# Attention score matmuls of two heads issued alternately, in pairs of tiles, with norm sums and scores sharing three PSUM banks

## The reference

```
h = RMSNorm(x);   q/k/v of all groups, z_A, z_B, g_A, g_B = split(h @ w_in)
q, k: RMS norm per head (64 wide)
Mixer A: 3 groups x 8 heads, query t reads t - j*d, j = 0..window/d, (window, d) = (128,1), (512,4), (2048,16)
         the three group outputs are added with weights proportional to their softmax denominators
Mixer B: 8 query heads, 2 kv heads, query t reads t-128..t, one sink logit per head in the denominator
scores = q.k / 8 - slope * distance;  p = softmax(scores);  o = p @ v
y = x + W_out( sig(g_A) * (o_A * silu(z_A)) @ P_A + sig(g_B) * (o_B * silu(z_B)) @ P_B )
```

## Time and profile before

| | |
|---|---|
| runs of the kernel before | 2306.69, 2309.11 and 2353.67 us, median 2309.11 us |
| the profiled execution's own time | 2317.27 us |
| span of its slowest core (core 3) | 2315.7 us |
| spans of the eight cores | 2283.2 to 2315.7 us |
| busy on core 3: PE, DVE, ACT, POOL | 1887.8, 1258.6, 1226.0, 428.7 us |
| mean granted TensorE clock, core 3 | 0.913 of full speed |

### The profile page before, as it was taken

How to read it: one execution, slowest core, us unless ns; L and a number is a source line. 1 busy time by engine, 2 the same in 40 slices (tenths; PEclk the granted TensorE clock), 3 DMA queues, 4 the chain that set the end, 5 groups by cost and what they waited for, 6 DMA issues and landing times.

```text
span 2315.7 us, 43826 instructions; the slowest of 8 cores (2283.2 to 2315.7 us)
## 1 busy us (share of the span) xinstructions
PE 1887.8 (82%) x14352; PEld 1073.0 (46%) x14352; DVE 1258.6 (54%) x1948; ACT 1226.0 (53%) x2190; POOL 428.7 (19%) x519
## 2 busy tenths in 40 slices
PE   3676576798698987988889887785786999999995
PEld 1453453464455544555555544342333445444442
DVE  3454254545355553554545545664565677776773
ACT  3544365577476864767657766775787311111110
POOL 0122001112112130121311212321222111111110
PEclk8798778899899998999999998887898999999997
DMA  7498753599757896659964696779455568777764
GB/s 171 130 227 198 141 163 104 146 185 183 170 143 166 177 181 163 167 139 203 181 160 153 163 193 128 155 152 164 124 132 136 171 189 232 218 214 199 200 174 128
DMA packets 133998, 389.20 MB, mean 168 GB/s; under 512 B 15488, under 2 KB 87696, under 8 KB 129520
## 3 DMA queue, kind: packets, MB, share of 16 engines
q10 hardware_dynamic: 5680, 178.06, 33.4%
q1 hardware_dynamic: 97024, 119.95, 19.3%
q0 software_dynamic: 31072, 88.39, 18.6%
HBM read 363.23 MB, written 230.06 MB: 256 GB/s over the span
## 4 chain that ended last, share of the span: by engine, by line
PE 56%; ACT 14%; DMA 13%; issue 9%; DVE 6%; ACTq 1%; POOL 1%; DVEq 0%; SPq 0%; POOLq 0%
PE ps L53 56%; ACT nl L53 6%; DMA xT<-scr_x 4%; DMA rw<-win 3%; ACT expt L53 2%; DMA sa<-ra 2%; ACT sq L53 2%; ACT ld L53 1%; ACT rb L53 1%; DVE tt L53 1%; DVE rd L53 1%; DVE pt L53 1%; DVE ra L53 1%; DMA ld<-x 1%; DVE rb L53 1%
## 5 line engine op out<-in xcount | busy, mean ns | idle before, releaser
L53 PE MATMUL ps<-xT,rw 128*128 128x512 bf16 x2496 | 672.9, 406 | 27.8 <-DMA xT<-scr_x 21.4
L53 DVE TENSOR_TENSOR pt<-expt,mask 128x512 bf16<-128x512 f32 x512 | 388.7, 772 | 273.8 <-ACT expt L53 249.8
L53 ACT ACTIVATE expt<-ps 128x512 f32<-128x512 f32 x576 | 334.3, 595 | 156.1 <-PE ps L53 117.0
L53 PEld LDWEIGHTS ps<-xT,rw 128*128 128x128 bf16 x2496 | 252.9, 106 | 286.1 <-issue 87.2
L53 PE MATMUL ps<-ra,rd 64*128 64x128 bf16 (+2 forms) x1792 | 281.2, 280 | 93.3 <-ACT expt L53 52.6
L53 ACT ACTIVATE sq<-ps 128x512 bf16<-128x512 f32 x257 | 149.3, 581 | 237.5 <-PE ps L53 237.2
L53 ACT ACTIVATE nl<-ps,epsS 128x512 f32<-128x512 f32 x257 | 174.9, 680 | 154.4 <-PE ps L53 150.1
L53 PE MATMUL ps<-rw,xT 128*128 128x128 bf16 x3328 | 228.9, 228 | 28.5 <-DMA rw<-win 15.9
L53 PEld LDWEIGHTS ps<-ra,rd 64*128 64x128 bf16 (+1 forms) x1792 | 127.8, 102 | 267.2 <-issue 202.6
L53 PEld LDWEIGHTS ps<-rw,xT 128*128 128x128 bf16 x3328 | 217.3, 122 | 36.9 <-issue 30.2
L53 ACT ACTIVATE nl<-nl 128x512 f32<-128x512 f32 (+1 forms) x321 | 200.8, 626 | 29.8
(11 more groups left out here) (134 smaller groups left out, 2212.3 us busy)
## 6 DMA issues: line engine op xcount, KB each, us to landing
xT<-scr_x SPq DMA_DIRECT2D x40, 1024.0 KB, 10.9
sa<-ca ACTq DMA_DIRECT2D x32, 1020.0 KB, 10.1
ra<-ca POOLq DMA_DIRECT2D x48, 512.0 KB, 6.9
rw<-win POOLq DMA_DIRECT2D x78, 256.0 KB, 14.8
rb<-x SPq DMA_DIRECT2D x32, 512.0 KB, 6.2
rb<-xh SPq DMA_DIRECT2D x16, 512.0 KB, 8.8
scr_x<-xT POOLq DMA_DIRECT2D x8, 1024.0 KB, 10.0
scr_ab<-ra SPq DMA_DIRECT2D x64, 128.0 KB, 4.8
```

Of the source, the lines that this page charges most:

```text
L53: return lambda eng: getattr(eng, name)(*args, **kwargs)
```

## The change

The score matmuls of a tile become a list of single steps (`s_mm`), and Exp and mask multiplication a separate part (`s_post`). `pair_heads` reorders each group's tiles so that tile i of head 0 and tile i of head 1 are neighbours in A. `do_tile` now issues two tiles at a time: their score matmuls in turn (head 0, head 1, head 0, ...), then both Exp and mask operations, then the `pv` parts with `LAG = 2`, which are those of the pair before. The planner deals out pairs (the account may reach 4, and 2 are taken off at a time). The norm sums and the scores take their banks from one rotation of the banks 3, 4 and 5, and the merge units keep the banks 4 and 5 in a rotation of their own.

```diff
-    rPJ = Rot([0, 1, 2]); NB = 3; rST = Rot([4, 5]); UA, UB = 6, 7
+    rPJ = Rot([0, 1, 2]); rST = Rot([3, 4, 5]); rMG = Rot([4, 5]); UA, UB = 6, 7
...
-            si, ni, b0 = st_["si"], rNL.next(), bank[0]
+            si, ni, b0, NB = st_["si"], rNL.next(), bank[0], rST.next()
...
-        def s():
-            stb = rST.next()
-            for ks, kap, qb, qap, c0, n in mms_s:
-                S.op(PE, lambda e: e.matmul(PS[stb][:, c0:c0 + n], lhsT=kap[rows, :], rhs=qap[rows, :], start=True, stop=True),
-                     reads=[ks.buf] + qb, writes=[b_PS[stb]])
+        def s_mm(m):
+            if "st" not in box:
+                box["st"] = rST.next()
+            stb = box["st"]
+            ks, kap, qb, qap, c0, n = m
+            S.op(PE, lambda e: e.matmul(PS[stb][:, c0:c0 + n], lhsT=kap[rows, :], rhs=qap[rows, :], start=True, stop=True),
+                 reads=[ks.buf] + qb, writes=[b_PS[stb]])
+
+        def s_post():
+            stb = box["st"]
...
+    def pair_heads(n0):
+
+        seg = A[n0:]
+        m = len(seg) // 2
+        A[n0:] = [t for p in zip(seg[:m], seg[m:]) for t in p]
+        for x in K1S + V1S + K2S + V2S + K3S + V3S:
+            if x.rd >= n0:
+                x.rd = len(A) - 1
...
-                ba[half] = rST.next()
+                ba[half] = rMG.next()
...
-    LAG = 3
+    LAG = 2
...
-        A[state["a"]].s()
-        state["a"] += 1
+        t0, t1 = A[state["a"]], A[state["a"] + 1]
+        for f0, f1 in zip(t0.s, t1.s):
+            f0()
+            f1()
+        t0.s_post()
+        t1.s_post()
+        state["a"] += 2
...
-            acc = min(acc + rate, 3.0)
-            while acc >= 1 and avail > 0:
+            acc = min(acc + rate, 4.0)
+            while acc >= 2 and avail > 1:
                 do_tile()
-                avail -= 1
-                acc -= 1
+                avail -= 2
+                acc -= 2
```

More of the change, by code:

```diff
@@ L425, in build_program, with __init__ @@
     class AT:
-        def __init__(self, after, s, pv, fin=None):
-            self.after, self.s, self.pv, self.fin = after, s, pv, fin
+        def __init__(self, after, s, s_post, pv, fin=None):
+            self.after, self.s, self.s_post, self.pv, self.fin = after, s, s_post, pv, fin
     M, A = [], []
@@ L767, in pv @@
                      reads=[vs.buf, b_PT[pi]], writes=[b_PS[ub]])
-        A.append(AT(after, s, pv, fin))
+        A.append(AT(after, [(lambda m=m: s_mm(m)) for m in mms_s], s_post, pv, fin))
         for x in [m[0] for m in mms_s] + [m[0] for m in mms_v]:
@@ L941, in build_program @@
             for r0 in range(0, 16, 4):
+                n0 = len(A)
                 for h in (0, 1):
@@ L945, in build_program @@
                               lambda r: (lambda ps: ps[:, 128 * r:128 * r + 128]), started, evac_g3(h, r0))
+                pair_heads(n0)
             qz_rd["q3"] = len(A) - 1
@@ L1148, in build_program @@
     ABS = RW.carve([128, 8, NS], BF16); b_ABS = S.buf("abs")
-    SQB, PU = 2, NB
+    SQB, PU = 2, 3
     b_small_s = [b_SGS, b_MIXS, b_ABS] + b_SC
```

## The result

The changed kernel takes 2363.85 us (median; the kernel before beside it 2307.9): ratio 1.0244, 95% interval 1.0185 to 1.0304. (All ratios here leave out the executions in which the cores of one half of the chip ran at a lower granted clock than the others.) Forecast were 2251 us and a range of 2205 to 2315. It is slower; whether by more than 2% is open. Its profiled execution has 2354.74 us; core 5 is now the slowest.

What follows compares the result with a forecast made beforehand. PE was taken to bound mixer A, and no engine alone mixer B. Of 110 us saved on PE, 46 in mixer A, 8 in mixer B and 4 in the first stretch remained: 58 us, from 2309 to 2251 us, range 2205 to 2315.

Steps and rivals of the forecast that it cites:

- The groups and the overlap: Score matmuls on PE: half as many groups saves 54 us, overlapping heads up to 57; 0.43 us per pair, 110 in all.
- "The sum", mixer A at 70 us: Mixer A, taken as PE-bound: 70 us saved on PE, less 15 and 9 given back, makes 46 us.
- "The read-out of banks 6 and 7 ... cover as long as a unit lies between": Both heads' readouts now come together; the next values stand a pair away, so no added wait was counted.
- What is given back by the lag, 47 us: PE waiting for PT at LAG 2: 29 us at 21 neighbouring pairs, 18 us at 30 pairs behind silu units.
- Banks at nothing: Shared rotation of three banks for scores and norm sums: same distance in tiles as before, costed at nothing.
- The clock: seen in a rival: The lag rival said idle gaps of PE would also lower its clock; the forecast sum had no term for this.
- C: Theory of the follow-up runs, not the prediction: overlapped matmuls lower the clock in mixer B, and that is the loss.
- The last stage unchanged: Stretch after 1800 us, without tiles: costed at nothing, its last 515 us to stay unchanged.
- The signs of being wrong: Mixer B much shorter, squares or banks 3 to 5 becoming what PE waits for, or the granted clock falling.
- "the lag decides": Rival, chance 0.13: PE waits for PT at each pair's values, some 130 us and more; total some 2340 us.
- x = 1.1: In the lag rival, us of waiting per pair with one unit between; from 1.1 the loss is over 2%, 2357 us.

Runs made afterwards that it cites:

- f3: Changed kernel with LAG 4 instead of 2 and eight PT buffers instead of four; ratio 0.9930.
- h1: Changed kernel with LAG 4, eight PT buffers and no pairing of heads, so a pair is two tiles of one head; ratio 0.9882.
- g3: Kernel before with norm sums and scores rotating through banks 3, 4 and 5, single tiles, LAG 5, eight PT buffers; 2266.99 us, ratio 0.9810.
- e4: Changed kernel with pair_heads left out in mixer B only, so a pair there is two tiles of one head; ratio 1.0099.
- g1: Changed kernel with a pair's two mask multiplications issued behind the value matmuls and readouts of the pair before; ratio 1.0324.
- h4: Changed kernel with the banks as before the change: norm sums in bank 3, scores in 4 and 5; ratio 1.0221.
- e2: Changed kernel with LAG 4 but still four PT buffers; PT was overwritten before use, so the output is not the layer's; ratio 1.3227.
- f1: Kernel before with only LAG set to 2: single tiles, no pairing, no alternation, two score banks; ratio 1.0179.
- e3: Changed kernel with a pair's score matmuls issued tile by tile (head 0, then head 1) instead of in turn; ratio 1.0248.
- g2: Changed kernel with LAG 4, eight PT buffers and a pair's score matmuls issued tile by tile instead of in turn; ratio 0.9889.

## Why the prediction was wrong, step by step

- **The groups and the overlap: right.** 0.43 us less per pair, half as many changes between 64 and 128 rows, eight matmuls in 0.34 us. PE's busy time over the span fell by 56 us and not by 110, in part since more of it ran at half clock. f3, with the same pairs, has most of the rest: its PE is busy 70 us less than before in mixer A (970 to 900, medians of the cores) and 27 in mixer B (269 to 242), where 0.43 us for each of the 192 and 64 pairs makes 83 and 28. The one write port into PSUM that the Trainium skill gives the array (TensorE: Matmul & The Clock Gate, Part 2) did not make the two heads take turns here: eight matmuls of both take as long as four of one.
- **"The sum", mixer A at 70 us: wrong, the step that failed most.** It let PE's saved time pass to the end of the stage, because PE was busy 87% of it. Mixer A was 3 us longer instead of some 50 shorter (46, and the 4 of its first stretch). The squares and Exp waited for in the earlier trace rows were read as a rest; with less work PE waits longer for them (103 us for the squares in mixer A in f3, 48 before, medians of the cores), which is the sign of a loop through ACT (argued from the waits, not tested by itself). Between f3 and h1 a third of PE's time shows in the stages and nothing in the totals; between f3 and g3 nothing shows at all. Even with the longer lag and the third bank, which alone gave 5 us there, f3's mixer A is only 22 us shorter than before.
- **"The read-out of banks 6 and 7 ... cover as long as a unit lies between": wrong, costed at nothing.** It is the largest new wait, 76 us over the span, at LAG 2 (e4, g1), and 18 at LAG 4 (f3).
- **What is given back by the lag, 47 us: too small, and under another name.** It was to show at pt, as 40 to 60 us; 18 us stood there. f3 has the changed kernel's pairs with the longer lag and is 25 + 55 = 80 us shorter in the two stages. In mixer B PE is idle 25 us less (130 to 105) and busy 30 us less, in mixer A 14 and 11; the waits for tt and pt fell, that for the squares rose. I had weighed the lag only against the one wait that it ends in directly.
- **Banks at nothing: right in the changed order** (h4), though alone they are a gain of 1.1%, which I didn't see.
- **The clock: seen in a rival, left out of the sum.** Half clock in mixer B rose from 96 to 146 us, and PE's busy time there stayed at 270 us, where f3's same instructions at 82 us of half clock take 242. By this estimate the clock accounts for up to 30 us of PE's time there. That overlapped matmuls bring the clock down (C) is not borne out: at the longer lag h1, without the overlap, has 101 us of half clock in mixer B, f3 with it 82 (e4's 110 at the short lag goes with less idle time too). Half clock rises with PE's idle time in the slow kernels, but not in step: f3 is idle 105 us in mixer B, the kernel before 93 with more half clock. So which comes first is not shown.
- **The last stage unchanged: right** (517 and 513 us).
- **The signs of being wrong** that the prediction named came: the granted clock fell, and the wait for the squares grew (83 to 99 us over the span).
- The rival "the lag decides", at 0.13, had the right side and named the lag, but not the mechanism: it wanted some 130 us and more of waiting for pt, and 18 us came. That its 2357 us at x = 1.1 lies near the 2364 measured is luck. Its evidence, the 2.8 us from scores to PT, was in the trace, and e2 bears it out.

The account of the change: pairing with alternation saves PE 110 us by the count of pairs, of which a third or less showed where it was put back; the short lag takes more than that, by itself 1.8% with single tiles (f1), and with pairs in good part through the common readout and along with a lower clock. What stays open is the share of the clock in mixer B's 41 us (no run holds it fixed), that of the transfer of xT in mixer A, and why single tiles with a lag of five do better than pairs with a lag of two pairs, where ratios are 0.9810 and 0.9930.

## What to carry to other kernels

An engine that is busy 87% of a stage and waits for the rest in short pieces on another that it feeds may be part of a loop: price the saving by what passes, not by what is saved, and test it by giving the time back, with everything else left in place, which h1 did not quite do. Where a change both shortens work and shortens the distance between producer and consumer, count every wait that the distance covers, buffer readouts on the third engine as well as the direct one. When buffers are cheap, try the distance first: here a third bank in the rotation, one number and eight small tiles (g3) did better than the changed kernel (1.0244) and than its pairs with the longer lag (0.9930).

## What the runs showed of the hardware

Matmuls on the two halves of the rows overlapped even when four of one head were issued before four of the other: 0.36 us for eight (e3), against 0.34 in turn (the changed kernel) and 0.57 on one half (h1). Over some 100 groups of eight with 128 columns on the slowest core of each the median is 0.40, 0.39 and 0.64 us. In e3 the eight records start in pairs 13 ns apart, where matmuls on one half start 55 ns apart or more (h1), so that the two of a pair are of different heads. The records don't name the head, and whether the chip took them out of the order of issue or ran the second four beside the first is not shown. The order in the program did not matter at this size (e3, g2).
